# Leaving the context tokens out of z, C, query and gate in the last layer of a two-block model

## The reference

```
p_lat = ada(x,   norm1, ...) @ w_in          # 512 tokens
p_ctx = ada(ctx, norm1, ...) @ w_in          # 256 tokens

# branch C, a state-space scan in chunks of 128 tokens
z, xbc, dt_f, dt_b = split(t, ...)           # for latent and for context
xbc = silu(depthwise_conv(xbc, width 5));  xs, B, C = split(xbc)
each chunk:  cum = cumsum(la)
             y = (C B^T * exp(cum_i - cum_j)) (x dt) + (C h) * exp(cum)
             h = h * exp(cum_last) + B^T (x dt exp(cum_last - cum))
out = rmsnorm((y_f + y_b + xs * d_skip) * silu(z))     # latent only

# branch D, gated linear attention in chunks of 64 tokens
q, k, v, g, gd = split(t, ...)
each chunk:  y = tril(q e^cum (k e^-cum)^T) v + (q e^cum) S
             S = S * e^cum_last + (k e^(cum_last - cum))^T v
out = rmsnorm(y_f + y_b) * silu(g)                     # latent only
```

## Time and profile before

| | |
|---|---|
| median of three runs | 4974.08 us (4967.86 to 4976.29) |
| the profiled execution's own time | 4968.61 us |
| its span in the profile | 4966.8 us |
| TensorE busy | 4148.3 us, 84% |
| VectorE busy | 2180.6 us, 44% |
| ScalarE busy | 1514.2 us, 30% |
| mean granted clock of TensorE | 0.903 |

### The profile page before, as it was taken

One profiled execution on the slowest core, in us unless ns is written; L12 is line 12 of the kernel. 1 busy time (PEld: TensorE's weight loads), 2 busy tenths in 40 slices (PEclk: granted clock), 3 DMA queues, 4 the chain that ended last, 5 costly groups with the idle time before them and its releaser, 6 DMA issues. The chain is left out here.

```text
span 4966.8 us, 71575 instructions
## 1 busy us (share of the span) xinstructions
PE 4148.3 (84%) x29590; PEld 3399.9 (68%) x29590; DVE 2180.6 (44%) x3607; ACT 1514.2 (30%) x2759; POOL 25.0 (1%) x45
## 2 busy tenths in 40 slices
PE   5988899979888999798948888799998457656998
PEld 4766777767666777666737777688877356545887
DVE  4474543336645333335464444433232543354434
ACT  4334422233443222325222222322222101333322
POOL 0000000000000000000000000000000000000000
PEclk8998999989998999879979998899999677767999
DMA  4331444323323433100100001111211001001332
GB/s 144 94 94 56 132 148 174 136 69 104 79 84 117 174 139 119 51 5 24 39 2 3 3 4 37 51 60 60 67 51 35 0 0 43 9 0 52 99 96 76
DMA packets 320251, 338.93 MB, mean 68 GB/s; under 512 B 25792, under 2 KB 298848, under 8 KB 313696
## 3 DMA queue, kind: packets, MB, share of 16 engines
q1 hardware_dynamic: 315808, 330.73, 20.9%
q10 hardware_dynamic: 4160, 4.19, 0.3%
HBM read 313.92 MB, written 20.97 MB: 67 GB/s over the span
## 5 line engine op out<-in xcount | busy, mean ns | idle before, releaser
L276 DVE TENSOR_TENSOR weights_lo<-weight_ring,weights_hi 128x1024 fp32r<-128x1024 f32 x370 | 453.2, 1225 | 1531.0 <-ACT weights_hi L272 1531.0
L272 ACT ACTIVATE weights_hi<-weight_ring 128x1024 fp32r<-128x1024 f32 x370 | 392.0, 1059 | 1772.6 <-PE banks L310 1684.0
L310 PE MATMUL banks<-mlp_x_lo,weights_hi 128*128 128x512 f32 (+1 forms) x1280 | 480.4, 375 | 0.0
L310 PE MATMUL banks<-mlp_hidden_hi,weights_hi 128*128 128x512 f32 (+1 forms) x1280 | 477.0, 373 | 0.0
L310 PE MATMUL banks<-mlp_hidden_lo,weights_hi 128*128 128x512 f32 (+1 forms) x1280 | 476.3, 372 | 0.0
L310 PE MATMUL banks<-mlp_hidden_hi,weights_lo 128*128 128x512 f32 (+1 forms) x1280 | 475.7, 372 | 0.0
L2391 PE MATMUL banks<-weight_ring 64*64 64x64 f32 x10368 | 342.1, 222 | 86.4 <-DVE weight_ring L2509 45.7
L2391 PEld LDWEIGHTS banks<-weight_ring 64*64 64x64 f32 x10368 | 321.2, 137 | 105.4 <-DVE weight_ring L2509 52.9
L310 PE MATMUL banks<-normed_hi,weights_hi 128*128 128x256 f32 (+1 forms) x992 | 355.1, 358 | 43.5 <-ACT normed_hi L290 39.8
L310 PE MATMUL banks<-normed_hi,weights_lo 128*128 128x256 f32 (+1 forms) x992 | 353.0, 356 | 0.0
L310 PE MATMUL banks<-mlp_x_hi,weights_hi 128*128 128x512 f32 x768 | 307.7, 401 | 27.0 <-DVE mlp_x_lo L296 27.0
(11 more groups left out here) (502 smaller groups left out, 7249.1 us busy)
## 6 DMA issues: line engine op xcount, KB each, us to landing
weight_ring<-in_w SPq DMA_DIRECT2D x64, 1024.0 KB, 5.4
mod_chunks<-in_mod_w SPq DMA_DIRECT2D x24, 2048.0 KB, 10.3
weight_ring<-in_w_in SPq DMA_DIRECT2D x41, 1024.0 KB, 5.3
weight_ring<-in_w_up SPq DMA_DIRECT2D x32, 1024.0 KB, 5.9
weight_ring<-in_w_down SPq DMA_DIRECT2D x32, 1024.0 KB, 5.0
weight_ring<-in_w_in SPq DMA_DIRECT2D x52, 512.0 KB, 4.2
weight_ring<-in_w_out SPq DMA_DIRECT2D x16, 1024.0 KB, 5.3
gate_logits_dram<-gates_staged SPq DMA_DIRECT2D x48, 256.0 KB, 4.4
```

Source lines behind the costliest of these rows:

```text
L272: act.activation(self.w_hi[:, t % 2], self._raw(t), ACT.Copy).then_inc(self.w_rounded, 1)
L276: dve.tensor_tensor(self.w_lo[:, t % 2], self._raw(t), self.w_hi[:, t % 2].bitcast(F32), ALU.subtract)\
L310: mm = pe.matmul(bank, a[:, k, :], b[:, k, t0:t0 + w], start=(k == 0 and n == 0), stop=(k == KD - 1 and n == 2))
```

## The change

`gemm` gets a list `latent_only` of tiles for which the context columns are neither multiplied nor copied out, and its loops are written out where such a list is given. Six of the 12 tiles of each projection are in it. The convolution, its sigmoid and the product start at column 258 for the two tiles of C. In a context step of the state-space scan the C B^T product, the squares and everything made from them are left out; the sum over the chunk, which was read out of the squares, is now a matmul with ones. In a context turn of the linear-attention scan the score product, its mask, and three of four exponentials' products are left out. Semaphores are raised by two where a step is gone.

```diff
 def multiply(...):
             for (t0, w), bank in zip(spans, banks):
+                if bank is None:
+                    continue
...
-    def banks(t):
+    def banks(t, tile=None):
         b = t % room * len(spans)
-        return [ps[:, b + s, 0:w] for s, (_, w) in enumerate(spans)]
+        return [None if s == 0 and tile in latent_only else ps[:, b + s, 0:w] for s, (_, w) in enumerate(spans)]
+
+    def repeat(eng, first, end, turn):
+        if latent_only:
+            for i in range(first, end):
+                turn(i)
+        elif end > first:
+            with eng.Fori(first, end) as i:
+                turn(i)
...
             gemm(kit, "ssm_project", w_in[:, :, 0:SSM_COLS], SSM_COLS, h, T2, store,
-                 low_place=low_place, fetch=fetch)
+                 low_place=low_place, fetch=fetch, latent_only=(0, 1, 2, 3, 10, 11))
...
+            def start(c):
+                return CTX + 2 if c >= 6 else 0
...
-                            src = raw[:, SSM_X + c, n:n + WS]
+                            src = raw[:, SSM_X + c, n + start(c):n + WS]
...
 # state-space scan, TensorE
-                        for g in range(2):
+                        for g in range(2 if latent else 0):
                             mm = pe.matmul(ps[:, 1, (2 + g) * P:(3 + g) * P], conv[:, 4 + g, at:at + P], ...)
-                        pe.wait_ge(dd, 1 + DVE_N * u + 1)
-                        pe.matmul(ps[:, 2, 0:8], mask, la[:, c, 8 * d:8 * d + 8], start=True, stop=True)
-                        for hd in range(8):
+                        pe.wait_ge(dd, 1 + DVE_N * u + (1 if latent else 0))
+                        mm = pe.matmul(ps[:, 2, 0:8], mask, la[:, c, 8 * d:8 * d + 8], start=True, stop=True)
+                        if not latent:
+                            mm = pe.matmul(ps[:, 2, 8:16], kit.const("ones"), la[:, c, 8 * d:8 * d + 8], ...)
+                        for hd in range(8 if latent else 0):
 # ScalarE
                         act.wait_ge(dd, 1 + DVE_N * u + 2)
+                        act.activation(w_end[:, d, :], w_end[:, d, :], ACT.Exp)
+                        if c < n_ctx:
+                            act.activation(end_decay[:, d, :], end_decay[:, d, :], ACT.Exp).then_inc(aa, 2)
+                            continue
                         act.activation(grown[:, d, :], cum[:, d, :], ACT.Exp)
-                        act.activation(w_end[:, d, :], w_end[:, d, :], ACT.Exp)
 # VectorE: la_wide, the eight lmat operations, cb and the lmat product only "if latent"
...
+        gemm(kit, "gla_project", w_in[:, :, AT_GLA:AT_GD], 1536, h, T2, store, fetch=fetch,
+             latent_only=(0, 1, 8, 9, 10, 11))
...
 # linear-attention scan
+                        if part == 0:
+                            pe.wait_ge(t.act.done, t.act.before(turn))
+                            pe.wait_ge(t.dve.done, t.dve.value(turn, "bd"))
-                        for name in t.pe.names:
+                        for name in t.pe.names[1 - part:]:
...
-                        act.activation(t.exps[:, 0], t.args[:, 0], ACT.Exp)
-                        act.activation(t.exps[:, 1], t.args[:, 0], ACT.Exp, scale=-1.0)
+                        if part == 1:
+                            act.activation(t.exps[:, 0], t.args[:, 0], ACT.Exp)
+                            act.activation(t.exps[:, 1], t.args[:, 0], ACT.Exp, scale=-1.0)
...
-                        for n, src, e in (("qa", GLA_Q, 0), ("ka", GLA_K, 1), ("qe", GLA_Q, 2), ("ke", GLA_K, 3)):
+                        for n, src, e in products if part == 1 else products[3:]:
...
-                        for name in t.dve.names:
+                        for name in t.dve.names if part == 1 else ("args", "bd", "state"):
```

More of the change, by code:

```diff
@@ L312, in multiply, with gemm @@
         return mm
-def gemm(kit, name, weights, n_cols, rhs, tokens, evacuate, engine="scalar", following=None, settle=None, **places):
+def gemm(kit, name, weights, n_cols, rhs, tokens, evacuate, engine="scalar", following=None, settle=None, latent_only=(), **places):
     ph, ps = kit.ph, kit.ps
@@ L345, in _ @@
                 full = n // 4
-                if full > 1:
-                    with sp.Fori(1, full) as i:
-                        turn(i, 2)
+                repeat(sp, 1, full, lambda i: turn(i, 2))
                 turn(full, n % 4 // 2)
@@ L365, in _ @@
                 full = n // 4
-                if full > 1:
-                    with pe.Fori(1, full) as i:
-                        turn(i, False)
+                repeat(pe, 1, full, lambda i: turn(i, False))
                 turn(full, False, n % 4)
@@ L388, in turn @@
                             evacuation(act, i, t)
-                with act.Fori(0, turns) as i:
-                    turn(i, 4, 4)
+                repeat(act, 0, turns, lambda i: turn(i, 4, 4))
                 turn(turns, rest, rest - 2)
@@ L408, in turn @@
                             settle(dve, i, t)
-                with dve.Fori(0, turns) as i:
-                    turn(i, 4, 4)
+                repeat(dve, 0, turns, lambda i: turn(i, 4, 4))
                 turn(turns, rest, rest - 2)
@@ L2765, in _ @@
                         dve.wait_ge(bent, c + 1)
-                        dve.tensor_tensor(conv[:, c, :], conv[:, c, :], tmps[:, c % 2, :], ALU.mult).then_inc(gated, 1)
+                        out = conv[:, c, start(c):]
+                        dve.tensor_tensor(out, out, tmps[:, c % 2, start(c):], ALU.mult).then_inc(gated, 1)
                     for c in range(4):
@@ L2786, in _ @@
                             act.wait_ge(gated, c - 1)
-                        act.activation(tmps[:, c % 2, :], conv[:, c, :], ACT.Sigmoid).then_inc(bent, 1)
+                        act.activation(tmps[:, c % 2, start(c):], conv[:, c, start(c):], ACT.Sigmoid)\
+                            .then_inc(bent, 1)
                     for c in range(4):
@@ L2894, in _ @@
                         spread = ps[:, 3:5, :].rearrange("p b (h n) -> p (b h) n", n=P)
+                        total = spread[:, :, last:last + 1].rearrange("p h n -> p (h n)") if latent else ps[:, 2, 8:16]
                         chain(dve.tensor_copy(cum[:, d, :], ps[:, 2, 0:8]))
-                        chain(dve.tensor_copy(end_decay[:, d, :], spread[:, :, last:last + 1].rearrange("p h n -> p (h n)")))
-                        dve.tensor_tensor(w_end[:, d, :], end_decay[:, d, :], cum[:, d, :], ALU.subtract).then_inc(dd, 1)
-                        for hd in range(8):
-                            ins = dve.tensor_scalar(lmat[:, d, hd, :], spread[:, hd, :], cum[:, d, hd:hd + 1], 0.0,
-                                                    ALU.subtract, ALU.min)
-                        ins.then_inc(dd, 1)
+                        chain(dve.tensor_copy(end_decay[:, d, :], total))
+                        dve.tensor_tensor(w_end[:, d, :], end_decay[:, d, :], cum[:, d, :], ALU.subtract)\
+                            .then_inc(dd, 1 if latent else 3)
+                        if latent:
+                            for hd in range(8):
+                                ins = dve.tensor_scalar(lmat[:, d, hd, :], spread[:, hd, :], cum[:, d, hd:hd + 1], 0.0,
+                                                        ALU.subtract, ALU.min)
+                            ins.then_inc(dd, 1)
                         dve.wait_ge(aa, 1 + ACT_N * u + 2)
@@ L3123, in step @@
                                                start=False, stop=True)
-                    mm.then_inc(t.pe.done, 1)
+                    mm.then_inc(t.pe.done, 2 if part == 0 and name == "turned" else 1)
                 for t in dirs:
@@ L3177, in _, with step @@
             def _(dve):
-                def step(t, turn, at, name):
+                def step(t, turn, at, part, name):
                     m = t.big
@@ L3207, in step @@
                         ends = t.exps[:, 2, :, end:end + 1].broadcast_to([P, 2, P])
-                        dve.tensor_tensor(m["state"], m["state"], ends, ALU.mult).then_inc(t.mid, 1)
+                        dve.tensor_tensor(m["state"], m["state"], ends, ALU.mult).then_inc(t.mid, 2 - part)
                         dve.wait_ge(t.mid, turn * 2 + 2)
                         ins = dve.tensor_tensor(m["state"], m["state"], bank(t, 3), ALU.add)
-                    ins.then_inc(t.dve.done, 1)
+                    ins.then_inc(t.dve.done, 2 if part == 0 and name == "bd" else 1)
                 for t in dirs:
@@ L3220, in _ @@
                         turn = i + part * (CTX // 64)
-                        for name in t.dve.names:
+                        for name in t.dve.names if part == 1 else ("args", "bd", "state"):
                             for t in dirs:
-                                step(t, turn, offset(t, part, i), name)
+                                step(t, turn, offset(t, part, i), part, name)
         half = ring[:, 0:4 * SEQ].rearrange("p (c n) -> p c n", c=4)
```

54 lines of the change are left out of this document (33 added, 21 removed).

## The result

| | before | after |
|---|---|---|
| median (lowest to highest) | 4972.14 us (4967.86 to 4976.29, 4 runs) | 4882.41 us (4879.24 to 4885.13, 4 runs) |
| span of the profiled execution | 4966.8 us | 4881.5 us |
| mean granted clock of TensorE | 0.903 | 0.905 |
| TensorE, VectorE, ScalarE busy | 4148.3, 2180.6, 1514.2 us | 4093.8, 2141.1, 1503.0 us |

The ratio is 0.9822, with a 95% interval from 0.9806 to 0.9837: 89.7 us less by the medians, somewhere from 81 to 96. The spans differ by 85.3. The forecast was 4887, with 86.1 us to come off.

A forecast was written before the change was run, and what follows sets the result against it. Projections were taken as bound by TensorE's matmuls, scans by chains of hand-offs between engines. Gains of 34.8 + 3.0 + 26.0 + 22.3 = 86.1 us from 4974.1 gave 4888; predicted 4887, range 4873 to 4902, with fetch stalls to 4907.

The forecast's parts named there:

- the forecast's own case: Whole kernel: every block's gain arrives as priced, 86.1 us off, median 4887 us; chance 0.80.
- Projections: Both projections: 2.86 us less for each of five tiles, 3.1 for the first tile; 34.8 us for both.
- the rival of the weights: Projections: something keeps latent-only tiles at 8.42 us, so 34.8 us are lost, median 4923; chance 0.04.
- that of the clock: Projections: fewer columns per tile leave TensorE at half clock, 57 us net slower, 5031; chance 0.02.
- Instruction fetch: Projections' written-out loops: forecast took no cost; the rival had 3.9 us per turn, 15.6 in all, 4904, chance 0.05.
- State-space context: State-space scan, four context steps: 8.2 us a step, 33.4 instead of 59.4 us, 26.0 gained.
- The bare wait: State-space context step: VectorE's x by dt stands behind ScalarE's exponentials, no longer covered by the squares; charged 0.9 us.
- Linear-attention context: Linear-attention scan, four context turns: 8.15 us a turn, 32.6 instead of 54.9 us, 22.3 gained.
- the 1.10 for `out`: Linear-attention context turn: from `out` to the state update, four half-clock passes charged at 1.10 us instead of 0.95.
- The upper bound of 25: Linear-attention context turns: 25 us gained if ScalarE's saving is whole and the clock stays.
- the 10 us that the range kept for it: State-space latent steps: another clock mixture could move them up to 1.26 us a step, 10 us either way; zero taken.
- a clock that moves away from 0.70: Sign of being wrong: the latent steps' granted clock leaves 0.70; they were to stay at 21.3 us each.

The follow-up runs named there:

- the second: The unchanged changed kernel timed once more against before, in another comparison: 4887.26 us, ratio 0.9826.
- filler: Changed kernel with idle transposes of the identity, whose result nobody reads, put into TensorE's gaps in both scans: 4863.43 us, ratio 0.9777.
- the loops written out: Kernel before with only the loops of the last layer's two projections written out: 4973.19 us, ratio 1.0008.
- the scans alone: Changed kernel with all projection tiles whole again, as loops, and the convolution over all columns: 4923.84 us, ratio 0.9911.
- more filler: Changed kernel with x by dt moved, the table load out of the turn, and higher counts of idle transposes: 4846.05 us, then 4834.48 us with the highest.
- the edits: Changed kernel with x by dt ahead of the sums and the exponential's table loaded ahead of the linear-attention loops: 4881.56 us, ratio 0.9819.
- the filled kernels: Idle transposes in both scans, added to the kernel before (4914.46 us) and, at the highest counts, to the changed kernel with the edits (4834.48 us).

## Why the prediction was right

The median came 4.6 us below the forecast of 4887 in the first comparison and 0.3 above it in the second. It is the forecast's own case that held, with its mechanism in each block that it put a price on, and none of the rivals.

**Projections, 34.8 forecast, 33.6 measured.** A cut tile takes 5.60 instead of 5.56 us, a whole one 8.48 in the first projection and 8.44 in the second instead of 8.42. The loops written out are not the reason, since kernels with loops have 8.48 in the first projection too; measured against those (106.6 us), the first projection gained 17.2 of the 17.4. The first tile of the first projection gave 2.8; the forecast's own sum for it, 11.2 less 8.3, is 2.9, and 3.1 was taken. There is no wait for weights and the clock is 1.00, which leaves nothing for the rival of the weights or for that of the clock. The Trainium skill ("TensorE: Matmul & The Clock Gate", Part 1: The HAM clock gate) has the low clock as the default that activity releases. The traces agree on both sides: 0.50 in the context steps that lost their matmuls, 1.00 in the projection whose matmuls follow without a gap, and 0.94 in the context turns that got filler.

**Instruction fetch, costed at nothing.** Right: no stall, projections as long as those of a kernel with loops (106.6 us), and the whole from -1 to 8 us against the rival's 15.6.

**Convolution, 3.0 forecast, 2.9 measured.**

**State-space context, 26.0 forecast, 25.4 measured.** The step is 8.43 instead of 8.2. The bare wait was there: with x by dt taken out from behind it the step is 7.65. Two hand-offs were sized too short. From the first of the sums' three small operations on VectorE, which start 0.20 and 0.28 apart (3907.49, 3907.69, 3907.97), to the end of the last exponential it is 0.98 and not 0.9: the exponential that went saved next to nothing. And x dt by the end weights starts 0.79 after x by dt and not 0.69, since it reads what that has just written. The forecast also dropped 0.07 where it rounded 4.6 + 0.06 + 2.11 to 6.7.

**Linear-attention context, 22.3 forecast, 20.9 measured.** This is the largest miss, 1.4 us. The term that failed is the 1.10 for `out`. It was made of three passes of 0.215 and a last one of 0.42, "as C B^T's row of 1.06 shows". But this group of four passes takes 1.33 at half clock to its reader, 0.23 more, which is up to 0.9 us over the four turns. The trace of before had a better row for it, the four-pass score products of the same loop, which was not used:

```profile
4349.54 1.23 PE L3103 MATMUL banks<-weight_ring 128*128 128x128 f32 x4 [5.62 <-DVE weight_ring L3196]
```

The other 0.08 a turn lie ahead of `out`, most of them between the transposes and ScalarE's copy, and the first turn is 0.25 longer than the rest. The reason given for the longer `out`, that TensorE would have worked too little to leave half clock, is shown by the filler for this group: 0.71 with it. For the whole turn it went too far, since the clock was 0.60 in the mean; that this changed nothing, because the second direction's `out` is not on the chain, was luck. The upper bound of 25 does not come out of its own terms either: 0.18 and 0.15 less a turn make 23.6.

**Costed at nothing, and not nothing.** The latent steps' clock moved from 0.70 to 0.68 and 0.9 us were lost, the linear-attention latent turns lost 0.6, both well inside the 10 us that the range kept for it. The forecast named a clock that moves away from 0.70 as a sign of being wrong; 0.02 is no more than what the same latent code does between traces, where it was 2.9 us longer with the loops written out. The block for the decays became 1.8 us shorter: 0.3 by the projection's last emptying (0.60 instead of 0.87), 0.6 by its transfer, which landed in 1.85 instead of 2.43 us, and 0.9 by its first matmuls, which came while the clock was still up (0.80 instead of 0.54). Only the first follows from the change. With the scans alone and with the loops written out the last tile is whole as before, and the block was 1.4 and 1.5 us shorter all the same. The losses and this gain nearly cancel, so the total came out better than its terms, and that is luck.

**The total.** The sum of 86.1 stands beside 85.3 of the spans, of which 1.9 is a luckier start, and 83.4 from the layer's start on. Its hits are thus real to 3%, and the last 3 us of agreement in the medians are luck: two comparisons of the same kernels gave 89.7 and 85.9.

## What to carry to other kernels

In a stretch where engines hand one step round, write down the chain of before in offsets and rebuild it operation by operation: that gave both scans' gains here to about 0.3 us a step, and it shows which wait loses its cover when work is cut. Take the price of a group of matmuls from a row with the same shape, the same number of passes and the same clock, and expect the clock to fall where the cut work was TensorE's. Then look for waits that were harmless under the removed work (one line moved: 0.8 us a step). Before a single trace's tenths are put down to an edit, measure the same block in a kernel that does not have the edit. And try filler on TensorE in such stretches, which here was worth more than half of what the change itself was.

## What was not expected of the hardware

Work that nobody reads makes the kernel faster. The granted clock of the state-space latent steps rose from 0.68 to 0.84 and 0.96 with more filler, and their time fell from 171.2 to 150.2 and 132.5 us; all four scan parts together gave 47 us of 4882. The kernel before gained 58.7 in the same way. So a part of what the change saves is the cost of the low clock on the removed matmuls: from the layer's start the change with the edits is worth 79.9 us between the filled kernels and 88.7 without filler.

The start of the same layer, behind identical code, differed by 7 us between traces (3736.10 to 3743.12). What causes it was not tried.
